# Projection tiles 4 to 27 computed in pairs by seven block products, with the weight sums made on GpSimd

## What is computed

```python
h = layer_norm(x)                       # (320, 1024)
u = h @ w_in                            # 1024 x 14720 columns, 115 tiles of 128 columns
# tiles 0-25: RWKV-7 part, mixed with the previous token: us = u + (shifted(u) - u) * mu
# tile 26: two low-rank parts; tiles 27-50: Mamba-2 x/B/C; then z, GLA, merge gates
```

## Time and profile before

| | us |
|---|---|
| median of 3 runs | 1502.66 (1501.89 to 1505.04) |
| span of the profiled execution | 1502.1 |
| TensorE busy | 1457.5 (97%) |
| of it matmuls of line 576, 1808 instructions | 510.2 |
| VectorE busy | 647.1 (43%) |
| ScalarE busy | 390.4 (26%) |
| GpSimd busy | 116.8 (8%) |
| granted TensorE clock, mean | 0.996 of 2.4 GHz |

### The profile page before, as it was taken

How to read it: one execution, slowest core, us unless ns; L and a number is a source line. 1 busy time by engine, 2 the same in 40 slices (tenths; PEclk the granted TensorE clock), 3 DMA queues, 4 the chain that set the end, 5 groups by cost and what they waited for, 6 DMA issues and landing times.

```text
span 1502.1 us, 31068 instructions
## 1 busy us (share of the span) xinstructions
PE 1457.5 (97%) x13071; PEld 1011.2 (67%) x13071; DVE 647.1 (43%) x1227; ACT 390.4 (26%) x874; POOL 116.8 (8%) x107
## 2 busy tenths in 40 slices
PE   7999999999999999999999999999999999999995
PEld 6776667677776777767766765766666767675751
DVE  5223778875644677734541114622211112121228
ACT  2112444442322554435431011111111111111111
POOL 3000113121010000000000000000000001000000
PEclk9999999999999999999999999999999999999998
DMA  7778375563344544565577538689999999999985
GB/s 243 168 174 181 101 214 166 132 203 97 103 130 147 138 112 116 178 180 163 135 231 263 157 100 359 251 337 399 417 423 430 428 426 429 426 428 429 427 342 211
DMA packets 157017, 375.27 MB, mean 250 GB/s; under 512 B 101708, under 2 KB 110300, under 8 KB 139216
## 3 DMA queue, kind: packets, MB, share of 16 engines
q1 hardware_dynamic: 123712, 341.35, 63.9%
q10 hardware_dynamic: 26592, 15.49, 3.5%
q0 software_dynamic: 6576, 16.48, 3.2%
HBM read 327.14 MB, written 51.95 MB: 252 GB/s over the span
## 4 chain that ended last, share of the span: by engine, by line
PE 82%; DVE 7%; DMA 4%; ACT 2%; DVEq 2%; issue 1%; SPq 1%; ACTq 1%; POOLq 0%
PE PS L576 27%; PE PS L1069 14%; PE PS L919 8%; PE PS L1036 7%; PE PS L1088 6%; PE PS L624 4%; PE PS L1041 2%; PE PS L957 2%; DVE region L1492 2%; DVE region L1499 2%; PE PS L632 1%; ACT L1172 1%; PE PS L1052 1%; PE PS L1077 1%; PE PS L817 1%
## 5 line engine op out<-in xcount | busy, mean ns | idle before, releaser
L576 PE MATMUL PS<-h0T,region 128*128 128x320 f32 x1808 | 510.2, 437 | 1.0 <-issue 0.8
L576 PEld LDWEIGHTS PS<-h0T,region 128*128 128x128 f32 x1808 | 336.8, 190 | 144.6 <-issue 12.2
L1172 ACT ACTIVATE region<-PS 128x9 f32<-128x9 f32 (+6 forms) x407 | 148.5, 383 | 681.9 <-PE PS L576 311.8
L1069 PE MATMUL PS<-region 128*64 128x512 f32 x1024 | 228.8, 592 | 0.0
L1069 PEld LDWEIGHTS PS<-region 128*64 128x64 f32 x1024 | 124.5, 137 | 92.2 <-issue 31.9
L1492 DVE TENSOR_TENSOR region<-region 128x256 f32<-128x256 f32 (+10 forms) x210 | 127.0, 624 | 96.8 <-ACTq L1218 76.2
L919 PE MATMUL PS<-region 128*128 128x320 f32 x512 | 138.6, 433 | 1.3 <-DMA region<-wo 1.2
L919 PEld LDWEIGHTS PS<-region 128*128 128x128 f32 x512 | 97.0, 190 | 42.5 <-issue 1.7
L1172 ACT ACT_TABLE_LOAD x80 | 102.6, 1283 | 73.1 <-DMA region<-projected 56.7
L1088 PE MATMUL PS<-region,history 128*64 128x512 f32 x512 | 119.7, 596 | 1.0 <-ACTq L1454 0.7
L1172 ACT ACTIVATE region<-region 128x256 f32<-128x256 f32 (+8 forms) x160 | 81.2, 531 | 147.9 <-DMA region<-projected 37.0
(11 more groups left out here) (210 smaller groups left out, 1163.8 us busy)
## 6 DMA issues: line engine op xcount, KB each, us to landing
region<-moe_w SPq DMA_DIRECT2D x64, 2048.0 KB, 17.4
region<-moe_w SPq DMA_DIRECT2D x64, 1024.0 KB, 15.0
region<-w_in SPq DMA_DIRECT2D x115, 512.0 KB, 5.6
region<-wo SPq DMA_DIRECT2D x32, 512.0 KB, 3.6
projected<-region ACTq DMA_DIRECT2D x65, 167.5 KB, 3.9
expert_rows<-region SPq DMA_DIRECT2D x20, 512.0 KB, 7.2
region<-expert_rows SPq DMA_DIRECT2D x5, 2048.0 KB, 14.4
region<-projected SPq DMA_DIRECT2D x10, 768.0 KB, 6.3
```

Of the source, the lines that this page charges most:

```text
L576: last = mm(PS[:, 6 + i % 2, 0:NTOK], WR[:, i, k, :], H0T[:, k, :], start=(k == 0), stop=(k == KT - 1))
L1069: last = mm(PS[tiles(i), 2, :], XE[:, k, tiles(i)], W13[r][i][:, k * 512:k * 512 + 512], start=(k == 0), stop=(k == KT - 1))
L1172: return nc.scalar.activation(out, in_, f, **kw)
```

## The change

A pair is two neighbouring tiles; its weights are seen as 2x2 blocks (tile a or b by the first or last four feature blocks) and the tokens as 2x2 blocks (features halved, each chunk of 64 tokens halved into 32 and 32). Seven products of 4 matmuls with 160 columns (28 matmuls, 56 instructions) replace the two tiles' 16 matmuls with 320 columns (32 instructions). For that

- VectorE forms four sums of token blocks once (`TSUM`, 640 columns each);
- GpSimd forms four sums of weight blocks for each pair (`weight_sums`, 512 columns each, with two inputs in SBUF), once both weight buffers have landed, and signals `weights_summed`;
- the products go to three PSUM banks (X, Z, W) for each parity of the pair. X is copied after one, two and three products; ScalarE copies (`keep`), VectorE adds the rest from PSUM (`quads`), so that the four output quarters end up in `STG`;
- the small copies (`edges`) and the mixing (`shift`) follow for both tiles, and a pair's stores are issued in the next pair's turn, behind its four copies (`tile_out`);
- the next loads are released by the fifth product (`freed`), from which on no buffer `WR` of the pair is read;
- `LNB` moves to memory that `USS` doesn't need, SP's wait for `h_kept` goes, and GpSimd's six row operations are done one at a time behind the weight sums of pairs 1 to 6;
- some semaphores are shared under new names.

```diff
+PAIRS = (PRE - RING) // 2
+        def quad_sum(b):
+            return shaped(PS[:, b, 0:NTOK // 2], NCH, L // 2)
+        def quad_out(i, j):
+            return STG[:, i, :, HIST + 32 * j:HIST + 32 * j + 32]
...
             with sp.Fori(1, 4) as m:
                 for i in range(RING):
                     weights(m, i)
-            sp.wait_ge(sem("h_kept"), 1)
             first_rows(0, 10)
...
+            def project_pair(m, u):
+                pair, a, b = m * 2 + u - 2, 2 * u, 2 * u + 1
+                X, Z, W = (quad_sum(3 * u + x) for x in range(3))
+                def product(out, lhs, rhs, start, freed=False):
+                    for k in range(KH):
+                        last = mm(out, lhs(k), rhs(k), start=start and k == 0, stop=k == KH - 1, skip_group_check=True)
+                        if freed and k < 2:
+                            last.then_inc(sem("tile_done"), 1)
+                    last.then_inc(sem("quad"), 1)
+                for i in (a, b):
+                    pe.wait_ge(sem(f"weights_in{i}"), (m + 1) * 16)
+                pe.wait_ge(sem("quads_out"), pair + 1)
+                product(X, lambda k: WR[:, a, k, :], lambda k: H0H[:, k, 0], True)
+                product(Z, lambda k: WR[:, b, KH + k, :], lambda k: TSUM[:, 3, k], True)
+                pe.wait_ge(sem("weights_summed"), pair + 1)
+                pe.wait_ge(sem("quad_kept"), pair * 4 + 1)
+                product(X, lambda k: WSUM[u][:, 1, k], lambda k: TSUM[:, 1, k], False)
+                pe.wait_ge(sem("quad_kept"), pair * 4 + 2)
+                product(Z, lambda k: WR[:, a, KH + k, :], lambda k: H0H[:, KH + k, 0], True)
+                product(W, lambda k: WSUM[u][:, 0, k], lambda k: TSUM[:, 0, k], True, True)
+                pe.wait_ge(sem("quad_kept"), pair * 4 + 3)
+                product(X, lambda k: WSUM[u][:, 2, k], lambda k: TSUM[:, 2, k], False)
+                pe.wait_ge(sem("quad_kept"), pair * 4 + 4)
+                product(W, lambda k: WSUM[u][:, 3, k], lambda k: H0H[:, KH + k, 1], False)
...
+            pe.wait_ge(sem("token_sums"), 1)
             with pe.Fori(1, PRE // RING) as m:
-                for i in range(RING):
-                    project(m, i)
+                for u in range(2):
+                    project_pair(m, u)
...
-            for n in range(PRE):
+            def keep(p, made, i, j, region):
+                act.wait_ge(sem("quad"), 7 * p + made)
+                a_(quad_out(i, j), region, ACT.Copy)
+                act.drain().then_inc(sem("quad_kept"), 1)
+            for n in range(RING):
                 move(n // RING, n % RING)
+            for p in range(PAIRS):
+                u, a, b = p % 2, 2 * (p % 2), 2 * (p % 2) + 1
+                act.wait_ge(sem("tile_mixed"), 2 * p + 2)
+                X, Z, W = (quad_sum(3 * u + x) for x in range(3))
+                keep(p, 1, a, 0, X)
+                keep(p, 2, b, 0, Z)
+                keep(p, 3, a, 1, X)
+                keep(p, 5, b, 1, W)
+                if p > 0:
+                    for n in (RING + 2 * p - 2, RING + 2 * p - 1):
+                        tile_out(n)
+                act.wait_ge(sem("quads_out"), p + 3)
+                for n in (RING + 2 * p, RING + 2 * p + 1):
+                    edges(n)
+                act.drain().then_inc(sem("tile_moved"), 2)
+            for n in range(PRE - 2, PRE):
+                tile_out(n)
...
+            def quads(p):
+                u, a, b = p % 2, 2 * (p % 2), 2 * (p % 2) + 1
+                X, Z, W = (quad_sum(3 * u + x) for x in range(3))
+                dve.wait_ge(sem("quad"), 7 * p + 4)
+                dve.wait_ge(sem("quad_kept"), 4 * p + 1)
+                tt(quad_out(a, 0), quad_out(a, 0), Z, add)
+                dve.wait_ge(sem("quad"), 7 * p + 6)
+                dve.wait_ge(sem("quad_kept"), 4 * p + 4)
+                for j in range(2):
+                    tt(quad_out(b, j), quad_out(b, j), X, add)
+                dve.wait_ge(sem("quad"), 7 * p + 7)
+                tt(quad_out(a, 1), quad_out(a, 1), W, add)
+                dve.drain().then_inc(sem("quads_out"), 1)
-            for n in range(T_MISC):
+            for n in range(RING):
                 shift(n)
+            for p in range(PAIRS):
+                quads(p)
+                for n in range(RING + 2 * p, min(RING + 2 * p + 2, T_MISC)):
+                    shift(n)
...
+            def weight_sums(p):
+                u, a, b = p % 2, 2 * (p % 2), 2 * (p % 2) + 1
+                S1, S2, S3, S4 = (flat(WSUM[u][:, x]) for x in range(4))
+                A11, A12, A21, A22 = (flat(WR[:, i, k * KH:k * KH + KH, :]) for i in (a, b) for k in range(2))
+                for i in (a, b):
+                    pool.wait_ge(sem(f"weights_in{i}"), (p // 2 + 2) * 16)
+                if p > 1:
+                    pool.wait_ge(sem("quad"), 7 * p - 7)
+                ptt(S1, A21, A22, add)
+                ptt(S3, A11, A21, sub)
                 pool.drain()
-            nc.gpsimd.sem_inc(sem("h_kept"), 1)
+                ptt(S2, S1, A11, sub)
+                pool.drain()
+                ptt(S4, A12, S2, sub)
+                pool.drain().then_inc(sem("weights_summed"), 1)
+            kept = [(t, k) for k in range(2) for t in range(TT3)]
+            for p in range(PAIRS):
+                weight_sums(p)
...
+                if 0 < p <= len(kept):
+                    keep_rows(*kept[p - 1])
```

78 lines of the change are left out of this document (58 added, 20 removed).

## The result

The changed kernel takes 1517.1 us (median; 1516.0 to 1518.9) beside 1503.9 us for the kernel before on the same chip: a ratio of 1.0092, 95% interval 1.0074 to 1.0110. The forecast was 1503.4 us, the range 1495 to 1511. The result lies beyond both, on the slower side. The profiled execution of the changed kernel, the slowest of its four, spans 1517.1 us, 15.0 more than that of the kernel before; the traces are compared on that scale.

The account below looks back on a forecast made before the run. TensorE bounds the stage of tiles 4 to 27, busy 103.22 of 103.30 us. Terms of -3.0 (stage), -0.3 (tile 3) and +4.0 (end) give +0.7 us: forecast 1503.4 us, 8-in-10 range 1495 to 1511.

Parts of the forecast that it names:

- TensorE's part: Tiles 4 to 27: 56 instructions of 160 columns at 0.137 us, 7.67 us a pair instead of 8.61.
- Rival 3: Shorter matmuls cost like those of 192 columns: 9.2 us a pair, 1514 us; chance 0.05.
- GpSimd's part: Pairs 1 to 7: weight sums 5.5, row operation 2.5, loss to mixing 0.75, so GpSimd needs 8.75 us a pair.
- its own refutation: The prediction is wrong if pairs 2 to 7 run below 8.3 us.
- Rival 1: GpSimd keeps up, pairs run at 7.7 us, gain 11 less 2 to 4: 1493.5 to 1496 us; chance 0.30.
- The ring of weights: A pair's second weight load lands 7.2 us after issue, so a pair takes at least 7.95 us on average.
- Rival 2: Weight loads land late: 9.0 us a pair over the last four, 1510.6 us, milder forms from 1505.7; chance 0.26.
- ScalarE and VectorE within a pair: Last addition and copies end 1.7 us after pair start, hidden under products 1 and 2, 0.5 us spare: no cost.
- 0.3 us of gain for tile 3: Tile 3 no longer waits behind a mixing that GpSimd holds: about 0.3 us gained.
- Sum over the stage: Tiles 4 to 27: GpSimd sets the pace through pair 7, weight loads after; end at 134.6, 3.0 us earlier.
- What the end gives back: RWKV chunk 0's read waits for the later stores of tiles 24 and 25: price 4.0 us, 3.2 to 8.
- a sign of being wrong: The prediction is wrong if later stages lose or gain more than 1 us relative to the stage's end.

Follow-up runs that it names:

- number 3: Changed kernel with tile 3's store, and ScalarE's wait for its mixing, moved behind the first pair's four copies; 1514.2 us, ratio 1.0064.
- all four mends: Changed kernel: reads four loads later, tile 3's store behind pair 0's copies, row operations every second pair, last stores behind the third copy; 1506.9 us.
- Number 2: Changed kernel with the first two reads of rows four loads later in SyncE's queue; 1512.4 us, ratio 1.0055.
- Numbers 1 and 10: 1: kernel before, phase 1 stores behind the next two tiles' copies, 1512.0 us; 10: ScalarE copies tiles 24 and 25, changed kernel 1510.8, kernel before 1502.7.
- 38 fillers: 38 unused tiny matmuls added ahead: changed kernel 1518.5 us, all four mends 1505.0, all four mends with ScalarE's copy 1504.5.
- `a_direct`: Changed kernel with chunk 0 of tiles 24 and 25 copied by DMA from SBUF straight to USS, third read without them; 1512.7 us, ratio 1.0068.
- `a_copy`: Changed kernel with ScalarE copying chunk 0 of tiles 24 and 25 from CV to USS, third read without them; 1510.8 us, ratio 1.0049.
- `a_tail`: Changed kernel with the stores of pairs 7 and later issued behind the next pair's third copy instead of its fourth; 1513.2 us, ratio 1.0058.
- number 8: Tiles 24 and 25 copied by DMA from SBUF straight to USS: changed kernel 1512.7 us, kernel before 1506.9, all four mends 1503.5.
- `b_direct`: Kernel before with chunk 0 of tiles 24 and 25 copied by DMA from SBUF straight to USS; 1506.9 us, ratio 1.0017.
- `a_all_direct`: Changed kernel with all four mends and the DMA copy of tiles 24 and 25 straight to USS; 1503.5 us, ratio 0.9999.

## Why the prediction failed, step by step

**TensorE's part: right.** Two products of eight instructions started 1.09 us apart, 0.136 each (0.137 predicted), an undisturbed pair took 7.61 us (7.67). Rival 3 fell.

**GpSimd's part: right.** Pairs 4 to 7 took 8.4, 8.4, 9.0 and 8.7 (8.75 predicted), ended by line 2392. Pairs 2 and 3 took 7.6 and 7.7, under the 8.3 that the text had named as its own refutation, since pair 0 had run late and the sums had a head start (number 3). VectorE's additions from PSUM took 0.32 us unhindered, the operations of the mixing 0.9 to 2.5 where they were held (31 of 46) and 0.49 or 0.55 where not. That is the rule of the Trainium skill (SBUF — State Buffer, "Who interferes with whom"), and the trace agrees with it. Rival 1 fell.

**The ring of weights: too dear where no read lies in the queue.** Pairs 8 and 9 took 7.6 and 7.8 (7.95): their second loads landed 4.5 and 4.6 us after issue, where 7.2 was taken, so TensorE set the pace and not the ring. (The 6.1 that the text gives for the loads before is 6.0 in rows 11; nothing hangs on it.) Rival 2 named late loads and was nearest in sign, and right in part for pair 10 alone. There the second load came some 5 us later than its neighbours' pace: 1.6 of it was issue, behind the read in SP's queue, and 3.5 landing (8.0 us instead of 4.5). The rival's reason was the same bytes in less time, but over the stage the loads landed in 3.3 to 8.0 us (median 4.7), faster than the 6.0 of before. What made pair 10's slow isn't shown: in five of the six versions with all four mends, where no read stands ahead of them, the second load of this pair took 7.3 to 9.0 us too, and in the sixth it wasn't recorded.

**"ScalarE and VectorE within a pair": failed at pair 0, +4.8 us.** The working gave ScalarE 0.5 us to spare and looked only at pairs that follow pairs. Ahead of pair 0 stands a tile of the old form, whose store ScalarE waits for, behind a mixing that GpSimd holds. All rows for it were there; the prediction even counted 0.3 us of gain for tile 3 at that place. Of the 4.8 us 3.0 are the wait and 1.7 the lower clock behind it. Number 3 shows the cause (2.86 to 0.45 us) and that undoing it alone moves the stage's end by 0.7 us in the profiled execution (3.5 us of the median).

**"Sum over the stage", the reads in SP's queue: failed, about 5 us.** The forecast priced them at "nothing, but up to 2 us each". The text had the last store landing at T+12.6 and the loads due at T+13.6. For the second read T is the start of pair 7, 95.4: the last store was issued at T+7.7 instead of T+6.6 and landed at T+14.7 (103.12 + 6.96 = 110.08), so the loads behind the read left 1.6 us late. They then landed 3.5 us slower than those before them, product 3 came 3.3 us late, and the lower clock cost 1.8 more. Neither of these two had a term. Number 2 moved the read, and 5.1 us of pair 10 went with it. Of the stage's forecast, 3.0 us earlier, the trace shows 2.2 later: +4.8 and +5.1 for the two pairs, and some 4.7 back by the others.

**"What the end gives back": right in mechanism, too small in size.** From the end of the stage to the low-rank part it was 14.8 us, 9.6 before: 5.2, in the range of 3.2 to 8 but over the 4.0 taken. The term that was off is the stores' landing: the last one 8.35 us after its issue, where 6.0 was taken (5.2 to 8.6 in rows 13). The read made up for some of it, with 5.1 us instead of 6.4. Numbers 1 and 10 show the mechanism from both sides.

**No step at all for the clock and for the later stalls.** The prediction read the clock of 1.00 in rows 2 and gave no term for its fall, which costs 3.5 us inside pairs 0 and 10. At 175 us the distance to the kernel before had grown from the 7.4 of line 690 to 9.3: 1.9 us for the 6.8 at the lower level. From there to the end it grew by another 5.7, with a peak at 15.9 behind the two stalls shown. The text had named more than 1 us of later loss as a sign of being wrong, and here it is 7.6. Added up: 5.5 (stage and tile 3) + 1.2 (end) + 1.9 + 5.7 = 14.3, the distance from the +0.7 of the forecast to the +15.0 of the trace.

**What stays open.** The stalls show as "issue". A queue of instructions carries blocks of 16 KB (1.67 MB in 102 packets, by the page of either kernel; 103 in the three versions with 38 fillers). One is recorded right at either stall, but between 178 and 295 us one comes every 4 to 13 us, stall or none. The fillers show that the stalls hang on the place of the code. That the fetch of a block comes late is argued, not shown; no run changed it by itself. Also, the stage of the changed kernel scatters: three profiled executions with the same stage (the change, `a_direct`, `a_copy`) ended it at 139.8, 135.5 and 141.2, in good part by pair 10 (12.7, 10.2, 11.3). In the seven versions that keep the second read in its place, pair 10 took 10.2 to 14.0 us, so the 5 us of "Sum over the stage" are one draw of 2.6 to 6.4. And the profiled execution of `a_tail`, the slowest of its four, lost some 6 us to the kernel before between 800 and 1000 us, with two more falls of the clock, which wasn't followed up.

## What to carry to other kernels

- When an engine's program changes form, work out the seam: the last step of the old form and the first of the new share queues, and a wait that was harmless on an idle engine stands in front of the new critical copy.
- A store that is moved back moves every read that waits for it, and every load that is queued behind that read. Follow it through each queue to its last user, here the end of the phase, where handing the last tiles over inside SBUF (one ScalarE copy of 0.31 us) took the place of a store and a read. But a mend that adds a wait ahead of other work, as number 8 did, can cost as much as it wins.
- In this kernel, whose bound engine is 97% busy, a gap could cost more than its length (pair 0: 3.0 us of wait, 1.7 of lower clock), and gains upstream count only when the next seam lets them through: three of the four mends won nothing or little in the stage alone, and all of them with the copy won some 16 us over the change and 2.5 over the kernel before.

## Of the hardware, not expected

- TensorE's waits of 2.9, 3.1 and 4.1 us in the changed kernel were followed by stretches of 3.4 or 6.8 us at 1.2 GHz (64 matmuls of 64 columns: 1.99 us for 1.16). At the low-rank part 0.8 us (`a_tail`), 1.7 (`a_copy`) and 2.7 (`a_direct`) were not, 3.0 (`b_direct`) was. But the length of the wait doesn't tell by itself: the wait of 3.4 us in pair 10 of `a_copy` left the clock as it was, while one of 1.9 us in pair 0 of `a_all_direct`, stalls of 1.6 to 1.9 us in four versions and waits of 1.2 us between 950 and 975 us in four were followed by a fall.
- In dense small matmuls between 195 and 285 us TensorE stood still for 0.8 to 3.1 us with nothing that the profile shows to wait for. With 152 instructions far ahead, whose results nobody uses, one stall over 0.7 us was left there in each of three versions (0.75, 0.78 and 1.19), and none of the three was clearly faster for it.
- A copy of 2 x 64 columns from SBUF to SBUF by DMA landed 6.2, 8.1, 9.0 and 10.7 us after its issue in four kernels; the read of 6 tiles' rows from DRAM, issued 0.4 us ahead of it, took 4.0, 7.0, 7.4 and 8.1. The way inside SBUF was the slower one each time.
